# Stick-breaking attention: the decay is applied to the output block by block instead of to the scores

## The reference

```python
z = jnp.einsum('bqhd,bkhd->bhqk', qb, kb) * scale
mask = s_idx[None, :] < t_idx[:, None]
log_fail = jnp.where(mask, jax.nn.log_sigmoid(-z), 0.0)
after = lax.cumsum(log_fail, axis=3, reverse=True) - log_fail
log_a = jax.nn.log_sigmoid(z) + after
a = jnp.where(mask, jnp.exp(log_a), 0.0)
outs.append(jnp.einsum('bhqk,bkhd->bqhd', a.astype(v.dtype), vb))
```

## Time and profile before

| | |
|---|---|
| Runs, median (lowest to highest) | 2474.54 us (2473.89 to 2475.95) |
| Span of the profiled execution | 2472.2 us |
| PE busy | 2302.2 us, 93% of the span |
| DVE, ACT, POOL busy | 1605.7, 1113.8, 1172.9 us |
| Attention of the second block, with the last projection unit ahead of it | about 1245 to 1625 us |

### The profile page before, as it was taken

The page is one execution under the profiler, slowest core; times in us unless marked ns, Lnnn a source line. Parts: engine busy times, 40 slices in busy tenths (PEclk is TensorE's granted clock), DMA queues, the critical chain, the costliest instruction groups (busy, mean ns, idle before and its releaser), DMA issues. The chain is left out here.

```text
span 2472.2 us, 28763 instructions
## 1 busy us (share of the span) xinstructions
PE 2302.2 (93%) x10276; PEld 1784.7 (72%) x10276; DVE 1605.7 (65%) x1865; ACT 1113.8 (45%) x1783; POOL 1172.9 (47%) x834
## 2 busy tenths in 40 slices
PE   8988876989999999999979998897899999999999
PEld 6865654767888887887755664574688888888877
DVE  7888874387666666557835666646966665544587
ACT  5245554354444443322126666624666662222243
POOL 1000000358888777877512111123577777777732
PEclk9999988999999999999989999998999999999999
DMA  3211100413344347874200000031365669876412
GB/s 129 66 34 34 26 22 5 171 51 113 137 160 170 113 177 300 331 305 155 79 18 18 26 18 26 5 136 60 139 270 230 250 261 366 315 284 267 167 30 86
DMA packets 89166, 342.90 MB, mean 139 GB/s; under 512 B 22401, under 2 KB 23169, under 8 KB 76097
## 3 DMA queue, kind: packets, MB, share of 16 engines
q1 hardware_dynamic: 88368, 336.65, 36.4%
q10 hardware_dynamic: 656, 4.41, 0.5%
HBM read 224.16 MB, written 116.27 MB: 138 GB/s over the span
## 5 line engine op out<-in xcount | busy, mean ns | idle before, releaser
L1077 PE MATMUL ps<-operand,turn_weights 128*128 128x512 f32 x3192 | 735.4, 392 | 16.2 <-POOL turn_weights L730 5.5
L1077 PEld LDWEIGHTS ps<-operand,turn_weights 128*128 128x128 f32 x3192 | 600.2, 188 | 150.5 <-issue 14.4
L730 POOL TENSOR_TENSOR turn_weights<-turn_raw,turn_weights 128x512 fp32r<-128x512 f32 (+1 forms) x330 | 445.4, 1360 | 225.5 <-ACT turn_weights L1545 224.8
L1077 PE MATMUL ps<-hidden_operand,turn_weights 128*128 128x512 f32 x2268 | 517.1, 389 | 3.2 <-issue 1.5
L692 POOL TENSOR_TENSOR weight_hi<-weight_raw,zero_col 128x1024 fp32r<-128x1024 f32 (+1 forms) x39 | 78.0, 2000 | 896.0 <-PE ps L983 407.2
L1077 PEld LDWEIGHTS ps<-hidden_operand,turn_weights 128*128 128x128 f32 x2268 | 424.8, 188 | 95.3 <-issue 5.5
L2731 DVE TENSOR_TENSOR branch_out<-ps,branch_out 128x1024 f32<-128x1024 f32 x172 | 210.5, 1224 | 201.3 <-PE ps L1077 200.2
L1545 ACT ACTIVATE turn_weights<-turn_raw 128x512 fp32r<-128x512 f32 (+1 forms) x330 | 205.0, 624 | 267.1 <-PE ps L1077 252.2
L818 PE MATMUL ps<-input_hi,weight_hi 128*128 128x512 f32 x608 | 201.6, 413 | 25.1 <-DVE input_lo L2310 10.4
L818 PE MATMUL ps<-input_lo,weight_hi 128*128 128x512 f32 x672 | 211.3, 396 | 0.0
L818 PE MATMUL ps<-input_hi,weight_lo 128*128 128x512 f32 x608 | 190.4, 395 | 0.0
(11 more groups left out here) (353 smaller groups left out, 3550.6 us busy)
## 6 DMA issues: line engine op xcount, KB each, us to landing
hidden_operand<-hidden_kept SPq DMA_DIRECT2D x91, 1024.0 KB, 8.1
hidden_kept<-hidden_parts SPq DMA_DIRECT2D x54, 1024.0 KB, 8.8
hidden_kept<-hidden_parts SPq DMA_DIRECT2D x27, 1536.0 KB, 6.3
turn_raw<-w_ff SPq DMA_DIRECT2D x40, 512.0 KB, 4.2
turn_raw<-w_mlp SPq DMA_DIRECT2D x32, 512.0 KB, 4.3
turn_raw<-w_mlpd SPq DMA_DIRECT2D x32, 512.0 KB, 4.4
turn_raw<-w_ffd SPq DMA_DIRECT2D x20, 512.0 KB, 4.5
weight_raw<-w_out SPq DMA_DIRECT2D x16, 512.0 KB, 3.6
```

What stands on the lines that cost most here:

```text
L730: pool_.tensor_tensor(place(p, 1), place(p, 1, WT) if raw is None else raw, bits(place(p, 0)), ALU.subtract).then_inc(s["st_lo"], 1)
L1077: ins = mm(PS[:, b, :], weights(p, w, k), tokens(p, a, k), start=(FRESH[p] and k == 0 and step == 0), stop=(k == n - 1 and step == 2), ski ...
```

## The change

The key blocks now run from the first to the latest. A tile's weights are decayed within the tile alone: `weights` reads scores plus triangle products straight from the product memory. The decay by the later blocks is put on the output instead. `block_sums` multiplies the unsplit softplus `sb_e` with 64 columns of minus ones for each head (plain float32), into bank 4, where `block_decay` takes its Exp in place; DVE multiplies what the output `sb_out` has so far with it (`decayed`) and adds the tile's V product from bank 6 (`summed`). So `sb_later_sums`, its copy, its memset, `add_sums`, the kept head mean and the copy of the output out of bank 6 go. The 48 tiles of the four heads are one loop over N, in which the next head's first scores are issued during the last tile of the head before. V's transposes and the head means go to bank 5. Q and K are split by halves. The last projection unit before the attention is computed by halves of the queries (`first_q`), with V's transposes ahead of it and the first scores inside its second half. `pool_out` stands ahead of `evac2(1, 0)` on DVE. The order in a pass on PE is now scores, V product, block sums, triangle, pieces; on ACT `lse`, `block_decay`, `weights`. The seventh operand of the output projection is made at p = 5 instead of 8. What SP and POOL issue is as before.

```diff
-    return [(half, b, max(0, b * P - half * H2)) for half in range(2) for b in range(4 * half + 3, -1, -1)]
+    return [(half, b, max(0, b * P - half * H2)) for half in range(2) for b in range(4 * half + 4)]
...
-            unit(u + 2, 0, 4)
...
+            def first_q():
+                pe.wait_ge(s["w_split"], u + 3)
+                for h in range(2):
+                    for k in range(KD):
+                        if h and k == 4:
+                            z_pair(0)
                         for step, (w, a) in enumerate(((WH, INH), (WH, INL), (WL, INH))):
...
+                            last = mm(PS[:, 4 + h, :], w[:, 0, k * P:(k + 1) * P], a[:, k, h * H2:(h + 1) * H2],
                                       start=(k == 0 and step == 0), stop=(k == KD - 1 and step == 2))
...
+            def block_sums(N):
+                c, p = divmod(N, NP)
+                _, b, lo = PAIRS[p]
+                if b == 0:
+                    return
+                pe.wait_ge(s["sb_soft"], N + 1)
+                if N == 1:
+                    pe.wait_ge(s["bank_free"], U_QKV2 + 3)
+                else:
+                    pe.wait_ge(s["sb_mul"], sums_before(c, p))
+                for h in range(2):
+                    last = mm(PS[DH * h:DH * (h + 1), 4, lo:], NONE[:, 0:DH], EX[p % 2][:, h, lo:],
+                              start=True, stop=True, skip_group_check=True)
+                last.then_inc(s["sb_up"], 1)
+            def pv_pair(N):
+                c, p = divmod(N, NP)
+                _, b, lo = PAIRS[p]
+                pe.wait_ge(s["sb_exp"], N + 1)
+                if p == 0:
+                    pe.wait_ge(s["v2_ready"], 2 * c + 2)
+                if N:
+                    pe.wait_ge(s["sb_acc"], N)
+                for h in range(2):
+                    last = mm(PS[DH * h:DH * (h + 1), 6, lo:], V2[c % 2][:, b, DH * h:DH * (h + 1)],
+                              AW[p % 2][:, h, lo:], start=True, stop=True, skip_group_check=True)
+                last.then_inc(s["sb_pv"], 1)
...
-                z_pair(0)
-                for p in range(NP):
-                    if p + 1 < NP:
...
-                    tri_pair(p)
-                    sums_pair(p)
-                    if p:
-                        pv_pair(p - 1)
...
+            for N in range(4 * NP):
+                c, p = divmod(N, NP)
+                if N + 1 < 4 * NP:
+                    z_pair(N + 1)
+                if p == 2 and c:
+                    head_mean(2 * c - 1)
+                elif p in (4, 5) and c < 3:
+                    turn_v(c, p - 4)
+                elif p == 8:
+                    head_mean(2 * c)
+                if N:
+                    pv_pair(N - 1)
+                block_sums(N)
+                tri_pair(N)
+                if c < 3:
+                    pieces(c, p)
+                elif p:
+                    output_pieces(p)
+            pv_pair(4 * NP - 1)
...
+            def weights(N):
+                p = N % NP
+                lo, zb = PAIRS[p][2], 2 * (p % 2)
+                act.wait_ge(s["sb_cum"], N + 1)
+                if N >= 2:
+                    act.wait_ge(s["sb_pv"], N - 1)
+                act_.activation(AW[p % 2][:, :, lo:], PS[:, zb:zb + 2, lo:], ACT.Exp).then_inc(s["sb_exp"], 1)
+            def block_decay(N):
+                c, p = divmod(N, NP)
+                _, b, lo = PAIRS[p]
+                if b:
+                    act.wait_ge(s["sb_up"], sums_before(c, p) + 1)
+                    act_.activation(PS[:, 4, lo:], PS[:, 4, lo:], ACT.Exp).then_inc(s["sb_decay"], 1)
...
-                def later_sums(p):
-                    half, b, lo = PAIRS[p]
-                    l1 = PAIRS[p - 1][2]
-                    if b == 4 * half + 2:
-                        act.wait_ge(s["sb_tz"], 2 * c + half + 1)
-                    act.wait_ge(s["sb_up"], sums_before(c, p))
-                    copy(TS[:, :, l1:], PS[:, 4:6, l1:]).then_inc(s["sb_ts"], 1)
...
+            for N in range(4 * NP):
+                c, p = divmod(N, NP)
+                if N + 1 < 4 * NP:
+                    lse(N + 1)
+                if c < 3:
+                    if p in (4, 5):
+                        v2_copy(p - 4, c + 1, 5)
+                    elif p == 8:
+                        q2_hi(0, c + 1)
+                    elif p == 10:
+                        q2_hi(1, c + 1)
+                block_decay(N)
+                weights(N)
...
-                def add_sums(p):
-                    half, b, lo = PAIRS[p]
-                    N, zb = NP * c + p, 2 * (p % 2)
-                    if b == 4 * half + 3:
-                        dve_.memset(TS[:, :, 0:H2 - P], 0.0).then_inc(s["sb_tz"], 1)
-                        return
-                    dve.wait_ge(s["sb_cum"], N + 1)
-                    dve.wait_ge(s["sb_ts"], sums_before(c, p))
-                    if N >= 2:
-                        dve.wait_ge(s["sb_pv"], N - 1)
-                    tt(AW[p % 2][:, :, lo:], PS[:, zb:zb + 2, lo:], TS[:, :, lo:], ALU.add).then_inc(s["sb_add"], 1)
...
+            def decayed(N):
+                c, p, b, lo, o = sum_at(N)
+                if b:
+                    dve.wait_ge(s["sb_decay"], sums_before(c, p) + 1)
+                    dve.wait_ge(s["sb_acc"], N)
+                    tt(o, PS[:, 4, lo:], o, ALU.mult).then_inc(s["sb_mul"], 1)
+            def summed(N):
+                c, p, b, lo, o = sum_at(N)
+                dve.wait_ge(s["sb_pv"], N + 1)
+                if b:
+                    dve.wait_ge(s["sb_mul"], sums_before(c, p) + 1)
+                    tt(o, PS[:, 6, lo:], o, ALU.add).then_inc(s["sb_acc"], 1)
                 else:
...
+                    dve_.tensor_copy(o, PS[:, 6, :]).then_inc(s["sb_acc"], 1)
...
+            softplus(0)
+            for N in range(4 * NP):
+                c, p = divmod(N, NP)
+                split(N)
+                if p == 0 and c:
+                    evac2(2, c, 1)
+                elif p % 2 == 0 and p and c < 3:
+                    evac2((p // 2 - 1) // 2, c + 1, (p // 2 - 1) % 2)
+                elif p % 2 and p > 1 and c == 3:
+                    output_part((p - 3) // 4, c + 1, (p - 3) // 2 % 2)
+                if N:
+                    decayed(N - 1)
+                if p == 1:
+                    q2_lo(2, c)
+                elif p == 3:
+                    q2_lo(3, c)
+                    if c:
+                        head_norm2(2 * c - 1)
+                elif p == 9:
+                    head_norm2(2 * c)
+                    if c < 3:
                         q2_lo(0, c + 1)
...
+                elif p == 10 and c < 3:
+                    q2_lo(1, c + 1)
+                if N:
+                    summed(N - 1)
+                if N + 1 < 4 * NP:
+                    softplus(N + 1)
```

More of the change, by code:

```diff
@@ L1296, in pieces @@
[L1296 to L1314 removed]
+                last.then_inc(s["sb_z"], 1)
@@ L1334, in output_pieces, with pieces @@
+            def pieces(c, p):
+                hu, half = p // 2, p // 2 % 2
+                v = U_QKV2 + 3 * c + 3 + hu // 2
+                if p % 2 == 0:
+                    if half:
+                        pe.wait_ge(s["half_free"], 3 * c + hu // 2 + 1)
+                    else:
                         pe.wait_ge(s["w_split"], v + 1)
                         pe.wait_ge(s["bank_free"], v)
[L1336 to L1341 removed]
@@ L1399, in _ @@
-                pv_pair(NP - 1)
+                    if c == 0 and p == 0:
+                        pe.wait_ge(s["v2_ready"], 2)
+                for k in range(4 * (p % 2), 4 * (p % 2) + 4):
+                    for step, (w, a) in enumerate(((WH, INH), (WH, INL), (WL, INH))):
+                        last = mm(PS[:, 7, :], w[:, v % 2, k * P:(k + 1) * P],
+                                  a[:, k, half * H2:(half + 1) * H2],
+                                  start=(k == 0 and step == 0), stop=(k == KD - 1 and step == 2))
@@ L2943, in _ @@
+            decayed(4 * NP - 1)
+            summed(4 * NP - 1)
             output_part(2, 4, 1)
-            head_root(7)
-            head_scaled(7)
+            head_norm2(7)
             mix_lo(7, OB[3][:], 8)
```

536 lines of the change are left out of this document (213 added, 323 removed).

## The result

The changed kernel takes 2453.76 us in the median of four runs (2451.17 to 2456.19), the kernel before 2475.24 us (2473.89 to 2477.19): 21.5 us less, a ratio of 0.9909 (0.9895 to 0.9923). The forecast was 2422 us with 2409 to 2443 as its range, so the time lies 10.8 us above the range. The sign is right; the gain is less than half of the 52.8 us that the sum gave.

A forecast was written before the change was run, and what follows sets the result against it. PE, busy 93% of the span, was taken as the bound, losing 78.9 us in the attention to waits and low clock. Gains 13 + 4.7 + 6.4 + 7.8 + 20.9 = 52.8 gave 2422 us, range 2409 to 2443.

The forecast's parts named there:

- start: Start of the attention: waits for pooling outputs (3.7 us) and first Q (7.3 us) go; 5 us remain, gain 13.
- heads 0 to 2: Full softplus after three narrow passes waits 1.2 and 1.5 us; 3 us left a head, gains 4.7, 6.4 and 7.8.
- head 3: Last head: output projection operands on ACT and DVE still hold PE up; 12 us left of 32.9, gain 20.9.
- sum: Gains of start, heads 0 to 2 and head 3 added, nothing behind the attention: 52.8 us, giving 2422 us.
- 2 to 3 us of slack now: Full passes: DVE's subtraction beside POOL, 2.80 instead of 1.23 us, cost PE 1.8 us before and would be absorbed.
- Sums: Block sums on PE: float32 products for two heads cost about 1.0 us for 512 columns, no difference from split products.
- float32 sums in full: Rival, chance 0.03: the two heads' block sums don't overlap, +30 us, 2452 us; its mark is sums of 2 us.
- The waits move: Rival, chance 0.14: the chain through `decayed` to the sums leaves full passes little gain; 32 us won, 2443 us.
- The other signs of the forecast: No ACT wait before weights' Exp in full passes, 6.9 us passes, PE idle about 22 us, start clock near 1.0.
- no wait for the norm now: Head 3, p = 5: the seventh operand was to cost only 0.5 us, without waiting for the norm.
- A slip in the sum: PE's work in head 3: 11 piece groups of 9 products counted at 2.28 us each, by scaling 2.95.
- Behind the attention: After the last V product: last mean, norm and eighth operand, weight splits and residual reloads move along, gain 0.

The follow-up runs named there:

- A: The changed kernel, with POOL's projection weight splits also waiting until DVE has split the softplus of the tile behind the unit's end: 2420.03 us, ratio 0.9775.
- G: A with head 3's `head_norm2(6)` behind the last tile and the seventh operand's low part at p = 6 instead of 5: 2419.81 us, ratio 0.9769.
- I: A with DVE's subtractions and ACT's copies for six output projection operands in head 3 cut to 8 columns instead of 1024: 2415.73 us, ratio 0.9754.

## Why the prediction was wrong

Predicted gains against measured ones, in us. In A the collision with full tiles is taken away and nothing else in the program.

| part | forecast | after | A |
|---|---|---|---|
| start | 13 | 10.6 | 13.1 |
| heads 0 to 2 | 18.9 | -2.5 | 27.2 |
| head 3 | 20.9 | 15.8 | 14.5 |
| sum | 52.8 | 24.0 | 54.9 |

The windows here begin one pass later in heads 1 to 3 than those of the earlier trace rows, and so than the forecast's. Cut where the forecast cut, at the start of head 3 (1528.2 us before, and the second tile's scores at 1523.16 us after and 1488.69 in A), heads 0 to 2 gained 0.9 us after and 27.1 in A, and head 3 12.5 after and 14.7 in A.

- **The failed step** is the one in *Heads 0 to 2*: "After three passes narrow for PE (5.3 to 5.5 us each) comes a full softplus, at p = 3 and at p = 11: low part at t + 7.5 to 8.5 against PE's need at about 7.3; 1.2 and 1.5 us of wait." The two places are right, but the step prices only a chain that is late by itself, and puts POOL at nothing there. The late chain alone costs next to nothing: in A PE waits 0 us at p = 4 and 0.31 at p = 0. The collision with POOL, over A's passes, cost 4.5 to 6.0 us each (3.6 in head 3), 29.8 us for the six where the forecast had 8.1 in all. Two things are in it. At head 1's start 3.4 us are wait: both of DVE's operations are stretched by POOL's pair, 5.4 us instead of 1.9, where the earlier trace rows show one stretched subtraction. And 2.1 us are clock: the low part's products and the 12 pieces last 5.7 us instead of 3.6.

  The forecast had judged a stretched operation by PE's slack in a full pass ("falls into 2 to 3 us of slack now"). That slack is there: at p = 5 of head 3 a subtraction took 2.91 us beside POOL (1563.26 us), and the pass 6.13 us where A's takes 5.97. In heads 0 to 2 it was not even needed, since at p = 8 POOL begins when DVE is nearly done: at 1325.64 us DVE's subtraction has run for 0.51 of its usual 1.23 us, and it is POOL's operation that takes longer, 2.47 us. The slack is not there after three narrow passes, and to those the new tile order had moved the full tiles.
- The Trainium skill ("SBUF — State Buffer", Who interferes with whom) says that DVE and GpSimd share one pair of ports under an exclusive lock, held for a whole instruction, and that a DVE instruction with two SBUF inputs, or a cast in a two-port mode, contends for it. The trace agrees: each of DVE's two operations ends about its own length or less behind the POOL operation beside it. By that rule a full tile's split that meets POOL's start ends with POOL's second operation plus one subtraction, not one subtraction late: 1355.18 + 1.23 = 1356.41 us at head 1's start, and 1356.26 was measured.
- **Start**: 13 us forecast, 10.6 measured and 13.1 in A. "low part 7.8 to 9.4 (POOL splits weights then)" had the collision in it; 2.5 us of the pass are owed to it.
- **Sums**: right. 0.96 us for 512 columns; the forecast's rival with float32 sums in full, 2452 us, lies near the measured time, but its mark, sums of 2 us, is not there.
- **The waits move** (2443 us): its sign, PE waiting at the block sums for `decayed` in most full passes, is absent; there are four such waits in the stage, all in head 3. The 0.69 us operations are as forecast.
- **The other signs of the forecast**: ACT waits at most 0.34 us ahead of the weights' Exp in the full passes of heads 0 to 2 away from the collisions, and these passes last 6.65 us (6.9 forecast). PE's idle time in the five windows is 36.6 us instead of about 22 (14.2 in A), and the clock at the start is 0.86 (0.92 in A), not near 1.0.
- **Head 3**: mis-sized, 12.5 us in the forecast's own cut instead of 20.9, and 14.7 in A. The chain at its start was followed rightly. DVE's rows of A, whose scores of the second tile start at 1488.69 us:

```profile
1494.86 4.06 DVE L2385 TENSOR_TENSOR input_lo<-pool_u,input_hi 128x1024 fp32r<-128x1024 f32 x3 [1.42 <-ACT input_hi L1541]
1498.85 0.55 DVE L2873 CAST sb_softplus_hi<-sb_e 128x768 fp32r<-128x768 f32 x1
1499.43 0.96 DVE L2875 TENSOR_TENSOR sb_softplus_lo<-sb_e,sb_softplus_hi 128x768 fp32r<-128x768 f32 x1
```

The subtractions end 10.2 us and the split 11.7 us behind those scores, both as counted. In the kernel after it is 13.2 and 14.7 us, since the collision at p = 0 stands ahead. Not in the forecast was, besides, the low clock after p = 0: in A the second group of output pieces ends 25.2 us behind those scores instead of 22.1. Nor was the wait at p = 6 (2.87 us after, 3.04 in A) while DVE stands for ACT's copy of the seventh operand, where the forecast had "no wait for the norm now". Without that wait (G) p = 6 and 7 together are 3.1 us shorter. Together these are about the 6.2 us by which A's head 3 misses the forecast.
- **A slip in the sum**: 2.95 us scaled from 12 to 9 pieces is 2.21, not 2.28; for 11 groups this is 0.8 us, and it does not matter here.
- **Behind the attention** nothing changed: from the first output product to the end 844.5 us after, 844.7 before.

With POOL placed behind DVE, the forecast's 2422 us is met by 2420.0. That this was the sum's largest missing term is shown; it doesn't make the forecast for the kernel as it stood right, and that the two times meet so closely is luck: in A heads 0 to 2 gained 8.2 us more than forecast and head 3 6.2 less. A and G, at 2420 us, are 2.25% faster than before and 1.4% faster than the change as made.

## What to carry to other kernels

When a change reorders the work of one engine, look at what the engines that were left alone do at that time: a collision that was free beside a narrow tile cost 4.5 to 6 us beside a full one. Slack has to be judged at each place where the collision falls and not in the typical pass. Waits of PE can cost more than their length, since the granted clock may fall behind them: 2.1 us on top of 3.4 at head 1's start, but nothing behind the 2.87 us at p = 6 of head 3. Where the gain is under 4 us, compare the length of the stage in the traces beside the medians.

## What the runs showed of the hardware

- Beside POOL's two 128x1024 operations (1.89 and 2.4 to 2.7 us) DVE's cast of the same size took 2.09 us instead of 0.69 and the subtraction 3.27 instead of 1.23, while POOL's own lasted 1.89 and 2.69 us, against 1.89 and 2.40 alone. Where DVE's subtraction had begun first, POOL's operation was the one held up: 2.47 us instead of 1.89 at 1325.64 us after, and in the kernel before 3.26 instead of 2.40 at 1413.16 us, behind the subtraction of the earlier trace rows.
- Two float32 products with 64 outputs each, one for each head and written to the two halves of the output partitions, took 0.90 to 0.96 us together for 512 columns, less than four split products with 128 outputs (1.00 us).
- After PE waits of 1.12 and 2.57 us close together the granted clock was 0.50 for 4.9 us (kernel after, head 1); after one of 1.48 us at p = 0 of head 3, where PE had had few products, for 6.2 us (I). After single waits of about 3 us at one and the same place, p = 6 of head 3, it was 1.00 after 2.87 us (kernel after), and 0.70 for 5.8 us after 3.04 us (A).
